# Placing the high and low halves of the two weight slots at 0, 64, 256 and 288 bytes in a 512-byte line

## Time and profile before

| what | value |
|---|---|
| three executions | 2406.37, 2407.29, 2409.31 us |
| median | 2407.29 us |
| the profiled execution, first to last instruction (span) | 2406.4 us |
| instructions in it | 29717 |
| matmul records, weight loads | 11108, 11108 |
| mean granted TensorE clock | 0.998 |

### The profile page before, as it was taken

One profiled execution on the slowest core, in us unless ns is written; L12 is line 12 of the kernel. 1 busy time (PEld: TensorE's weight loads), 2 busy tenths in 40 slices (PEclk: granted clock), 3 DMA queues, 4 the chain that ended last, 5 costly groups with the idle time before them and its releaser, 6 DMA issues.

```text
span 2406.4 us, 29717 instructions
## 1 busy us (share of the span) xinstructions
PE 2379.8 (99%) x11108; PEld 1924.6 (80%) x11108; DVE 1209.2 (50%) x1961; ACT 965.8 (40%) x1513; POOL 1316.2 (55%) x1589
## 2 busy tenths in 40 slices
PE   8999999999999999999999999999999999999999
PEld 8777778888888888777787888888887777788887
DVE  5997765423224432379625743333325785266331
ACT  4554444322223223566524432332336764344321
POOL 5763246656556655366244765555554562466554
PEclk9999999999999999999999999999999999999999
DMA  5321123333333333222122333333332221223333
GB/s 166 109 71 53 47 77 97 96 97 97 97 97 110 97 97 103 71 72 69 54 87 79 97 97 97 96 97 97 97 98 67 72 78 53 88 87 98 96 97 96
DMA packets 59758, 213.40 MB, mean 89 GB/s; under 512 B 6624, under 2 KB 6752, under 8 KB 59488
## 3 DMA queue, kind: packets, MB, share of 16 engines
q1 hardware_dynamic: 59472, 211.38, 29.2%
q10 hardware_dynamic: 144, 0.14, 0.0%
HBM read 209.39 MB, written 2.10 MB: 88 GB/s over the span
## 4 chain that ended last, share of the span: by engine, by line
PE 91%; DVE 6%; issue 1%; ACT 1%; DMA 0%; POOL 0%; SPq 0%; DVEq 0%; ACTq 0%
PE banks L721 89%; DVE t L1203 1%; DVE t L1211 1%; DVE t L1213 1%; DVE t L1488 1%; DVE t L1204 1%; DVE t L1197 1%; DVE t L1219 0%; PE banks L841 0%; PE banks L995 0%; DVE t L1222 0%; ACT t L1679 0%; DMA t<-in_w 0%; PE banks L875 0%; POOL t L1992 0%
## 5 line engine op out<-in xcount | busy, mean ns | idle before, releaser
L721 PE MATMUL banks<-t,t 128*128 128x512 f32 (+4 forms) x10788 | 2351.7, 387 | 17.2 <-ACT t L1699 5.9
L721 PEld LDWEIGHTS banks<-t,t 128*128 128x128 f32 (+2 forms) x10788 | 1889.5, 188 | 452.2 <-issue 64.3
L1992 POOL TENSOR_TENSOR t<-t,t 128x256 fp32r<-128x256 f32 x1544 | 1258.9, 846 | 1049.9 <-ACT t L1679 1041.5
L1679 ACT ACTIVATE t<-t 128x1024 fp32r<-128x1024 f32 x385 | 408.2, 1060 | 1078.8 <-issue 605.5
L1197 DVE TENSOR_TENSOR t<-banks,t 128x512 f32<-128x512 f32 x121 | 83.1, 687 | 169.8 <-PE banks L721 169.2
L1378 DVE TENSOR_TENSOR t<-banks,t 128x512 f32<-128x512 f32 x44 | 30.4, 690 | 184.5 <-PE banks L721 184.3
L1346 DVE SCALAR_TENSOR_TENSOR t<-banks,t 128x512 f32<-128x512 f32 x32 | 22.1, 691 | 155.4 <-PE banks L721 155.4
L1080 DVE SCALAR_TENSOR_TENSOR t<-t,t,t 128x512 fp32r<-128x512 f32 x64 | 52.0, 817 | 58.1 <-ACT t L1699 58.1
L1323 DVE TENSOR_TENSOR t<-t,t 128x512 fp32r<-128x512 f32 x68 | 70.5, 1036 | 2.3
L1352 DVE TENSOR_TENSOR t<-banks,t 128x512 f32<-128x512 f32 x24 | 16.6, 691 | 106.0 <-PE banks L721 106.0
L1699 ACT ACTIVATE t<-t,t 128x512 fp32r<-128x512 f32 x64 | 45.6, 715 | 55.7 <-DVE t L1346 49.1
(11 more groups left out here) (182 smaller groups left out, 1304.7 us busy)
## 6 DMA issues: line engine op xcount, KB each, us to landing
t<-in_w SPq DMA_DIRECT2D x386, 512.0 KB, 3.5
t<-in_xT SPq DMA_DIRECT2D x8, 256.0 KB, 5.7
out<-t SPq DMA_DIRECT2D x8, 256.0 KB, 4.5
t<-in_dmask SPq DMA_DIRECT2D x1, 1536.0 KB, 7.7
t<-in_vbias SPq DMA_DIRECT2D x2, 384.0 KB, 4.1
t<-in_c SPq DMA_DIRECT2D x1, 576.0 KB, 8.6
t<-in_w SPq DMA_DIRECT2D x2, 256.0 KB, 3.9
t<-in_pos SPq DMA_DIRECT2D x2, 256.0 KB, 4.1
```

Source lines behind the costliest of these rows:

```text
L721: return pe.matmul(o, l, r, start=start, stop=stop, skip_group_check=True)
L1679: a.activation(whl[u % 2][:, 0:1024], wraw[u % 3][:, :], ACT.Copy).then_inc(*w_high.next(u))
L1992: p.tensor_tensor(hl[:, 1024:2048][:, c], wraw[u % 3][:, c], as_f32(hl[:, c]), ALU.subtract).then_inc(*w_low.next((u, q)))
```

## The change

The two tiles of 2048 columns become four of 1024, each with a gap of its own behind it. The high half of slot 0 begins 0 bytes past the place in a 512-byte line at which XH begins, the low half of slot 0 begins 64 bytes past it, the high half of slot 1 256 bytes and the low half of slot 1 288 bytes. The gaps add up to 512 bytes, so what lies behind the slots moves by 512 bytes and keeps its place in a line. All readers and writers of the slots take the new names; no instruction, size, wait or step is added or taken away.

```diff
-        whl = [take(2048, F32R) for _ in range(2)]
+        WH, WL = [], []
+        for u_ in range(2):
+            WH.append(take(1024, F32R))
+            top[0] += (64, 32)[u_]
+            WL.append(take(1024, F32R))
+            top[0] += (192, 224)[u_]
...
             def weights(n):
                 u, i = divmod(n, 8)
-                hl = whl[u % 2]
                 low_parts(need, u, i // 2)
-                return hl[:, 128 * i:128 * i + 128], hl[:, 1024 + 128 * i:1152 + 128 * i]
+                return WH[u % 2][:, 128 * i:128 * i + 128], WL[u % 2][:, 128 * i:128 * i + 128]
...
-                rh = whl[u % 2][:, 128 * i:128 * (i + n)]
-                rl = whl[u % 2][:, 1024 + 128 * i:1024 + 128 * (i + n)]
+                rh, rl = (of[u % 2][:, 128 * i:128 * (i + n)] for of in (WH, WL))
...
-                    a.activation(whl[u % 2][:, 0:1024], wraw[u % 3][:, :], ACT.Copy).then_inc(*w_high.next(u))
+                    a.activation(WH[u % 2][:, :], wraw[u % 3][:, :], ACT.Copy).then_inc(*w_high.next(u))
...
-                hl = whl[u % 2]
                 for q in quarters:
                     c = slice(256 * q, 256 * q + 256)
-                    p.tensor_tensor(hl[:, 1024:2048][:, c], wraw[u % 3][:, c], as_f32(hl[:, c]),
+                    p.tensor_tensor(WL[u % 2][:, c], wraw[u % 3][:, c], as_f32(WH[u % 2][:, c]),
                                     ALU.subtract).then_inc(*w_low.next((u, q)))
```

More of the change, by code:

```diff
@@ L1071, in half_weights @@
                 if u in FRONT:
-                    hl = whl[u % 2]
                     need.wait_ge(*w_high.at(("front", u)))
-                    v.tensor_tensor(hl[:, 1024:1536], wraw[u % 3][:, 0:512], as_f32(hl[:, 0:512]), S_).then_inc(
+                    v.tensor_tensor(WL[u % 2][:, 0:512], wraw[u % 3][:, 0:512], as_f32(WH[u % 2][:, 0:512]), S_).then_inc(
                         *w_low_front.next(u))
@@ L1676, in half_weights @@
                 if u in FRONT:
-                    a.activation(whl[u % 2][:, 0:512], wraw[u % 3][:, 0:512], ACT.Copy).then_inc(*w_high.next(("front", u)))
+                    a.activation(WH[u % 2][:, 0:512], wraw[u % 3][:, 0:512], ACT.Copy).then_inc(*w_high.next(("front", u)))
                 else:
-                    a.activation(whl[u % 2][:, 0:1024], wraw[u % 3][:, :], ACT.Copy).then_inc(*w_high.next(u))
+                    a.activation(WH[u % 2][:, :], wraw[u % 3][:, :], ACT.Copy).then_inc(*w_high.next(u))
             def half_weights_rest(u):
                 need.wait_ge(*in_w[u % 3].at(u))
-                a.activation(whl[u % 2][:, 512:1024], wraw[u % 3][:, 512:1024], ACT.Copy).then_inc(*w_high.next(u))
+                a.activation(WH[u % 2][:, 512:1024], wraw[u % 3][:, 512:1024], ACT.Copy).then_inc(*w_high.next(u))
             def load_cols():
```

## The result

The changed kernel took **2444.91 us** (median of four executions, 2444.71 to 2446.29) beside 2407.57 us for the kernel before in the same rounds: a ratio of 1.0152, 95% interval 1.014 to 1.0165, 37.3 us slower. The forecast was 2437 us, slower by 30.4 us.

The account below looks back on a forecast made before the run. PE was taken to bound the kernel through the distance between matmul starts. Steady stretches 24.0 us plus the others 6.4 us gave 30.4 us over 2407.3, rounded 2437 us; own range 2422 to 2453, whole range 2355 to 2470.

Parts of the forecast that it names:

- What bounds the kernel: Whole kernel: PE busy 2379.8 of 2406.4 us, so time is matmul count times start-to-start distance, 226.6 ns for 512 columns.
- The steady stretches: Three long dense stretches: 5990 matmuls, each 4.0 ns longer, add 24.0 us, all on the path.
- The others: 3214 matmuls of 512 columns between attention work: half of 4.0 ns each adds 6.4 us (bounds 0 and 12.9).
- ScalarE and GpSimd: The engines writing the weight slots: same sizes and counts, idle time to cover them, so 0 us.
- The 512 bytes by which all behind the slots moves: Everything in SBUF behind the slots: a shift at which weight blocks already differ without a trace in the distances, so 0.
- The step that failed: Dense triples: weight place changes at two of every three matmuls, so no settling was expected, at 4.0 ns a matmul.
- `sb_later`: Earlier trace, stationary pieces 64 bytes off: matmuls of 388, 398 and 393 ns averaged 393.0, giving the 4.0 ns price.
- Rival 1: Nothing changes: 2407 us, the 13.3 ns belonging to every full-rate matmul; chance 0.19.
- Rival 2: Faster: triples close one 13.3 ns step sooner, 4.4 ns a matmul, 41 us, 2366 us; chance of faster 0.35.
- 13.3 ns: Dense matmuls: distance of 226.6 ns over the 213.3 ns that 512 columns take; some 120 us over 9204 matmuls.
- Rival 3: Much slower: triples never settle and cost 9 ns a matmul like strided loads, 2490 us; chance 0.08 for over 60 us.
- a toll that the load takes from the matmul beside it: End of a steady run: a matmul without a load under it takes 388 like others, so the 13 ns are no such toll.

Follow-up runs that it names:

- (0, 0, 256, 256): Bytes past the input's place (high, low of slot 0; high, low of slot 1), set throughout the changed kernel: 2408.57 us, ratio 1.0002 to the kernel before.
- (0, 256, 256, 256): Same order of tiles, held for ten units in one run of the changed kernel with successive sets of places: 2429.9 us overall, 226.7 ns a matmul here.
- The table of prices: Start-to-start distances from four runs of the changed kernel, stepping all four weight tiles, low tiles, high tiles or slot 1 through 0 to 496 bytes: 2425.2 to 2444.1 us.
- low alone: Changed kernel with both high tiles at 0 and both low tiles stepped together through 0 to 496 bytes: 2433.3 us beside 2406.8 for the kernel before.
- the sweep: Changed kernel with the four tiles given successive sets of places, ten units each, the change's own among them: 2429.9 us beside 2406.8 for the kernel before.
- 126 sets: All places of the four weight tiles read in six runs of the changed kernel that re-place them every 10 to 12 units: none under 226.7 ns with 512 columns.
- slot 1 alone: Changed kernel with slot 0 at 0 and both halves of slot 1 stepped through 0 to 496 bytes: 2425.2 us beside 2406.8 for the kernel before.

## Why the prediction was right, and where it was not

*What bounds the kernel*: as read. Only the distance between matmuls moved, 226.6 to 231.9 ns, and the other engines' busy times stood still. Of the readings beside it, the 256-column distance is 120.0 by the starts, not 121, and the 428 ns for float32 is one of the two records that such a matmul leaves. Neither changes the sum.

*The steady stretches*, 5990 matmuls at 4.0 ns, 24.0 us: measured 31.0 us. The count took in 156 matmuls of fewer columns, so it is 5834 at 5.3 ns, and the price was 1.3 ns low. *The others*, half of that on 3214 (3370 by the same count), 6.4 us: measured 6.9. The half was a guess, and that it came out so well is luck. *ScalarE and GpSimd*, 0: their pieces took 845 and 1059 ns as before. The waits of PEld, which answer to the last line of the earlier trace rows:

```profile
PEld banks L726 <- POOL t L1993: 5.6, 7, 1.8
```

1.0 us less than before, so no part of the 37 us. *The 512 bytes by which all behind the slots moves*, 0: a whole number of periods of 256 bytes; the set (0, 0, 256, 256), with the same shift behind it, ran at a ratio of 1.0002.

*The step that failed* is the one before the sum: "one load in three of such a unit is at another place, so that the place changes at two of every three matmuls", and with it "As the place changes again in each triple, I expect no settling". Changes of place by 256 bytes cost nothing (a ratio of 1.0002 with slots 256 bytes apart; 389 at (0, 256, 256, 256), where high and low of slot 0 lie 256 bytes apart), and with no change of place at all, 64 bytes off, the kernel lost 46.7 us. The runs put a steady price in its place, set in the main by where the weights of a triple lie against the input modulo 256 bytes. The table of prices also gives the change: slot 0 holds (0, 64), low alone at 64, 231.1; slot 1 holds (256, 288), which is (0, 32), low alone at 32, 233.3. The mean is 232.2; the sweep read 232.1 at the change's own set and the changed kernel 231.9. My row for the price, `sb_later`, was rightly seen as the place's doing and wrongly as the change's. Its two matmuls, 398 and 393, are what the kernel with all four tiles at 64 bytes shows in its steady stretch, in turn and without end (two neighbours, 604.28 to 604.33 and 604.51 to 604.56 us):

```profile
L727 PE MATMUL banks<-t,t 128*128 128x512 f32 x1 | 0.4, 398 | 0.0
L727 PE MATMUL banks<-t,t 128*128 128x512 f32 x1 | 0.4, 393 | 0.0
```

So those two alone, 6.5 ns over 389, would have given the steady price of 64 bytes (6.7), and the 388 ahead of them, which I averaged in, had no part in it. That the row is the steady pattern rests on two matmuls and is likely, not shown. The forecast's 4.0 ns came near the measured 5.3 by luck: it is a diluted price of one place, and the change happens to mix places with prices of 4.4 and 6.7 over its two slots.

*Rival 1*, nothing changes, fell. With four sets of places and no other difference, the runs gave ratios from 1.0002 to 1.0196. The Trainium skill, "TensorE: Matmul & The Clock Gate", section on what happens when you issue a matmul, says that two independent read ports keep a load of weights from taking bandwidth from the running matmul. The measurement decides against what I drew from that, that the place can then do nothing; whether a load takes bandwidth away from the places that cost isn't shown, since no matmul ran there without its load. *Rival 2*, one step of 13.3 ns fewer in each triple, fell for this kernel's time. Its step may be real all the same: by the starts, 70 of the 126 sets lie at 226.7, 228.9, 231.1 or 233.3 ns, rungs of 2.2 ns, 13.3 / 6 (102, 103, 104 or 105 steps over two triples; the others lie between or above them). None was under 102 with 512 columns. With 256 columns there was such a gain. In the value projections the weight slot is the moving operand, and in 938 to 944 us of the kernel before the starts are 120.0 ns apart. With all four tiles at 64 bytes (959 to 965 us) they are 117.8 apart, one step fewer over six matmuls:

```profile
L727 PE MATMUL banks<-t,t 128*128 128x256 f32 x53 | 6.4, 279 | 0.0
```

With some 150 such matmuls in the long stretches this is 0.3 us, so no time shows it. *Rival 3* at 9 ns was too dear, though all four at 64 came to 6.7. The earlier trace rows told against a toll that the load takes from the matmul beside it, and the free place bears that out: there the matmul reads 389 with a load under it and 388 without (one matmul).

What stays open: why the price is what it is at each place, and whence the 13.3 ns at the free place; why 3.3 ns come on top when the input itself lies at 16 or 240 bytes, and by what rule the low half of the input alone costs; and why slot 1 alone at 16 or 496 bytes ran at 226.7 where all four there took 233.3 and 228.3. The last looks like a pattern that holds on once it is entered, but no run tested that. Two more things weren't tried: matmuls at these places without any loads, and kernels made of 256-column streams.

## What to carry to other kernels

Where TensorE streams `float32r` back to back with a weight load for each matmul, put stationary and moving operands at the same place modulo 256 bytes in the partition, and take any odd-sized tile that comes ahead of them to a full line: being off it cost up to 2% here, and for streams of 512 columns no place was better. Streams of 256 columns gained 2.2 ns a matmul off that place; if a kernel lives on those, measure it there. When a price is read from a disturbed run, ask whether it is paid on the way into a state or in it, before it is multiplied by a count; one kernel that holds the state throughout (here, all four at 64) tells.

## What the runs showed that I had not expected

- The place of the weights against the moving input sets most of the pace of matmuls with 512 columns, with a period of 256 bytes: 226.7 ns at 0 and 256, 233.3 with all four tiles at 32, 64 or 288, up to 236.7 with the input at 240 ((85,000 + 400) / 361 gives 236.6).
- 4 bytes past the free place are enough (232.4 ns with all four at 4); 4 bytes ahead of it are not (226.7 at 252).
- With 256 columns, and the weight slot as the moving operand, the place that costs 6.7 ns at 512 columns saves 2.2.
- A load in the wrong place shows nothing itself. In the kernel with all four at 64, PEld by form in 500 to 600 us has the old duration:

```profile
L727 PEld LDWEIGHTS banks<-t,t 128*128 128x128 f32 x429 | 80.7, 188 | 19.4
```

  The price is visible only in the matmuls, and there only as a few ns on each: not as a wait, nor in the chain, nor in a busy share.
